# Moving the first gate's modulation rows of the second block from an output projection into the attention before it

## The reference, cut to what matters

```python
# first block, layer l
shift, scale, gate = jnp.split((s_lat @ w_mod[l] + b_mod[l])[:, None, :], 3, axis=-1)
...
x = x + gate * y
# second block
mod = jax.nn.silu(c) @ w_mod[l] + b_mod[l]
sh1, sc1, g1, sh2, sc2, g2 = jnp.split(mod, N_MOD, axis=-1)
...
x = x + g1[:, None] * (merged @ w_out[l])
```

## Time and profile before

| | us |
|---|---|
| median of 3 runs | 3005.51 |
| lowest and highest | 2998.6 and 3023.86 |
| time of the profiled execution | 3000.39 |
| its span in the profile | 2998.6 |
| second attention (layer 1), gate tile 1 to gate tile 15 | 1318.86 to 1444.55 |
| its output projection, from the third tile on | 1475.60 to 1556.35 |

### The profile page before, as it was taken

One profiled execution on the slowest core, in us unless ns is written; L12 is line 12 of the kernel. 1 busy time (PEld: TensorE's weight loads), 2 busy tenths in 40 slices (PEclk: granted clock), 3 DMA queues, 4 the chain that ended last, 5 costly groups with the idle time before them and its releaser, 6 DMA issues.

```text
span 2998.6 us, 48547 instructions
## 1 busy us (share of the span) xinstructions
PE 2857.1 (95%) x17809; PEld 2474.9 (83%) x17809; DVE 1784.0 (59%) x3201; ACT 1452.6 (48%) x2227; POOL 1827.7 (61%) x756
## 2 busy tenths in 40 slices
PE   6899999999899799999988999999999999999999
PEld 4688886777778798878877888999987888888888
DVE  2487982799788857548679998772325444442000
ACT  3222222566422532258645787665446555555443
POOL 1244443333333674455665777668787888888998
PEclk9899999999999899999988999999999999999999
DMA  9877321565687797233674444345565766665655
GB/s 400 318 266 271 142 98 68 201 209 187 230 307 289 250 360 283 84 121 119 229 290 134 158 165 152 136 146 176 168 203 174 246 230 232 239 215 191 208 205 188
DMA packets 147414, 621.50 MB, mean 207 GB/s; under 512 B 16288, under 2 KB 17616, under 8 KB 126288
## 3 DMA queue, kind: packets, MB, share of 16 engines
q1 hardware_dynamic: 146128, 614.48, 57.5%
q10 hardware_dynamic: 1152, 5.24, 0.4%
HBM read 617.54 MB, written 2.12 MB: 207 GB/s over the span
## 4 chain that ended last, share of the span: by engine, by line
issue 46%; POOL 29%; PE 24%; POOLq 1%; DVE 0%; DVEq 0%
POOL w_low L690 29%; PE bank L725 16%; PE bank L726 8%; POOLq L685 0%; POOLq L689 0%; POOLq L690 0%; DVE region L1825 0%; DVE region L1828 0%; DVEq L1825 0%; POOLq L2658 0%
## 5 line engine op out<-in xcount | busy, mean ns | idle before, releaser
L690 POOL TENSOR_TENSOR w_low<-raw,w_high 128x1024 fp32r<-128x1024 f32 x752 | 1827.5, 2448 | 1159.9 <-ACT w_high L1197 1156.8
L1197 ACT ACTIVATE w_high<-raw 128x1024 fp32r<-128x1024 f32 x752 | 793.0, 1057 | 794.9 <-PE bank L738 294.4
L736 PE MATMUL bank<-h,w_high 128*128 128x256 f32 (+1 forms) x2816 | 949.8, 337 | 15.6 <-POOL w_low L690 12.5
L737 PE MATMUL bank<-h,w_high 128*128 128x256 f32 (+1 forms) x2816 | 935.9, 332 | 0.0
L738 PE MATMUL bank<-h,w_low 128*128 128x256 f32 (+1 forms) x2816 | 935.6, 332 | 0.0
L736 PEld LDWEIGHTS bank<-h,w_high 128*128 128x128 f32 x2816 | 538.0, 191 | 92.7 <-issue 25.0
L725 PE MATMUL bank<-h,w_high 128*128 128x512 f32 x1664 | 583.9, 395 | 8.4 <-DVE h L1791 4.2
L738 PEld LDWEIGHTS bank<-h,w_low 128*128 128x128 f32 x2816 | 537.7, 191 | 51.0
L737 PEld LDWEIGHTS bank<-h,w_high 128*128 128x128 f32 x2816 | 538.3, 191 | 50.1 <-issue 0.7
L726 PE MATMUL bank<-h,w_low 128*128 128x256 f32 x1664 | 467.8, 281 | 0.0
L725 PEld LDWEIGHTS bank<-h,w_high 128*128 128x128 f32 x1664 | 313.5, 188 | 80.6 <-POOL w_low L690 4.6
(11 more groups left out here) (256 smaller groups left out, 3506.8 us busy)
## 6 DMA issues: line engine op xcount, KB each, us to landing
raw<-in_w_in SPq DMA_DIRECT2D x344, 512.0 KB, 3.6
raw<-in_w_up SPq DMA_DIRECT2D x176, 512.0 KB, 3.5
region<-in_w_rows SPq DMA_DIRECT2D x71, 1024.0 KB, 7.4
row_extra<-in_w_rows SPq DMA_DIRECT2D x57, 1024.0 KB, 6.9
raw<-in_w_out SPq DMA_DIRECT2D x96, 512.0 KB, 5.6
raw<-in_w_down SPq DMA_DIRECT2D x96, 512.0 KB, 3.4
row_extra<-in_w_half_rows SPq DMA_DIRECT2D x64, 512.0 KB, 4.3
region<-in_w_mods SPq DMA_DIRECT2D x28, 1024.0 KB, 9.6
```

Source lines behind the costliest of these rows:

```text
L690: nc.gpsimd.tensor_tensor(WL[s][:, part], RAW[s][:, part], WH[s][:, part], ALU.subtract) \
L736: nc.tensor.matmul(bank[:, 0:n], WH[slot][:, w], h, start=first and j == 0, stop=False)
L737: nc.tensor.matmul(bank[:, 0:n], WH[slot][:, w], l, start=False, stop=False)
L1197: return nc.scalar.activation(out, in_, func, **kw)
```

## The change

The 16 MB of rows for `g1` leave the stage `out1` and become a stage `att1`: 32 half rows, two behind each of the 16 steps of the second attention, in the manner of `att0`. The host lays them out as half rows. `ROW_ATT0`, the two halves of `ROW_EXTRA`, are the places again, and the conditioning vector goes into `ROW_OUT`, half of it before row 0 and the other half before row 16. SP's loop over units 40 to 53 is written out, with one unit behind each pair of rows; `w_out1` now goes by the plain loop of pairs. The output projection has no rows any more. The core of the diff:

```diff
-    ROW_STAGES = {... "out1": (ROW_OUT1, 18), "up": (ROW_UP, 18)}
+    ROW_STAGES = {... "att1": (ROW_ATT0, 32), "up": (ROW_UP, 18)}
...
+        def row_att1(e):
+
+            if e % 16 == 0:
+                sp.wait_ge(sem("row_used"), ROW_FIRST["att1"] + e)
+                sp.dma_start(ROW_OUT[:].unsqueeze(1), CONDS[:, 2:3, HALF * (e // 16):HALF * (e // 16 + 1)].broadcast_to([P, 1, HALF])) \
+                    .then_inc(sem("cond_rows"), 16)
+            row_load("att1", e, dram["w_half_rows"][64 + e])
...
+                for g in range(16):
+                    row_att1(2 * g)
+                    row_att1(2 * g + 1)
+                    if g < 14:
+                        one(40 + g)
+                return
...
-            if name == "w_out1":
-                two(0)
-                two(1)
-                row_out1(0)
-                sp.wait_ge(sem("at_y"), 12)
-                row_out1(1)
-                row_out1(2)
-                for t in range(4, 16):
-                    for e in range(t - 1, t + 3 if t == 15 else t):
-                        row_out1(e)
-                    one(t)
-                return
...
+        def rows_att1(e):
+
+            half, m = e // 16, e % 16
+            if m == 0:
+                dve.wait_ge(sem("cond_rows"), 65 + 16 * half)
+            place = row_landed("att1", e)
+            total = mod_col(128 + m, 2) if half else ROW_PART[:, m:m + 1]
+            V.scalar_tensor_tensor(place, place, 1.0, ROW_OUT[:], ALU.mult, ALU.mult, accum_out=total) \
+                .then_inc(sem("row_used"), 1)
+            if e == 31:
+                row_bias(ROW_ALL["att1"], 128, 16, 2, 3, 0).then_inc(sem("row_out"), 1)
...
-                if l == 0:
-                    rows_att0(2 * g)
-                    rows_att0(2 * g + 1)
+                for e in (2 * g, 2 * g + 1):
+                    rows_att0(e) if l == 0 else rows_att1(e)
...
-            else:
-                for e in range(3):
-                    rows_out1(e)
...
-                elif n < 15:
-                    rows_out1(3 + n)
```

More of the change, by code:

```diff
@@ L98, in lay_out @@
     out["w_rows"] = np.concatenate([rows_of(early, 0, 2), rows_of(early, 1, 2), rows_of(mods[96:128]),
-                                    rows_of(mods[128:144], 0, 2), rows_of(mods[128:144], 1, 2),
                                     rows_of(mods[176:192], 0, 2), rows_of(mods[176:192], 1, 2),
                                     *(rows_of(late, q, 4) for q in range(4))])
-    rows = rows_of(mods[144:176])
-    out["w_half_rows"] = np.concatenate([rows[:, :, :HALF], rows[:, :, HALF:]])
+    rows, more = rows_of(mods[144:176]), rows_of(mods[128:144])
+    out["w_half_rows"] = np.concatenate([rows[:, :, :HALF], rows[:, :, HALF:], more[:, :, :HALF], more[:, :, HALF:]])
     order2 = list(range(24, 32)) + list(range(24)) + list(range(32, 64))
@@ L341, in build @@
     ROW_IN1 = [ROW_EXTRA[:], *r2(4096, 6144)]
-    ROW_OUT1 = [ROW_EXTRA[:], *r2(0, 4096)]
     ROW_UP = [ROW_EXTRA[:]]
-    ROW_STAGES = {"in0": (ROW_IN0, 34), "att0": (ROW_ATT0, 64), "out0": (ROW_OUT0, 36), "in1": (ROW_IN1, 33), "out1": (ROW_OUT1, 18), "up": (ROW_UP, 18)}
+    ROW_STAGES = {"in0": (ROW_IN0, 34), "att0": (ROW_ATT0, 64), "out0": (ROW_OUT0, 36), "in1": (ROW_IN1, 33), "att1": (ROW_ATT0, 32), "up": (ROW_UP, 18)}
     ROW_FIRST, ROW_LANDED = {}, {}
@@ L532, in row_out0 @@
             else:
-                row_load("out0", e, dram["w_rows"][96 + 8 * (e // 9) + e % 9 - 1])
+                row_load("out0", e, dram["w_rows"][80 + 8 * (e // 9) + e % 9 - 1])
         def row_in1(e):
@@ L540, in row_in1 @@
                 row_load("in1", e, dram["w_rows"][32 + e - 1])
-        def row_out1(e):
-            if e % 9 == 0:
-                row_cond("out1", e, slice(2, 3), e // 9, 2)
-            else:
-                row_load("out1", e, dram["w_rows"][64 + 8 * (e // 9) + e % 9 - 1])
+        def row_att1(e):
[4 more added lines that the diff above has]
+            row_load("att1", e, dram["w_half_rows"][64 + e])
         def row_up(e):
@@ L553, in row_up @@
             else:
-                row_load("up", e, dram["w_rows"][80 + 8 * (e // 9) + e % 9 - 1])
+                row_load("up", e, dram["w_rows"][64 + 8 * (e // 9) + e % 9 - 1])
         row_in0(0)
```

## The result

The changed kernel takes 3140.54 us (median of 4 runs, 3134.75 to 3146.8) against 3014.69 for the kernel before in the same comparison (2998.6 to 3025.66): a ratio of 1.042, 95% interval 1.036 to 1.048. The forecast was 3142. The profiled execution took 3146.8 us with a span of 3145.0, against 3000.39 and 2998.6 before. By the profiles the loss is 146 us, by the medians 126: the execution profiled before was near the fastest of its kernel and the one profiled after was the slowest of its four.

What follows compares the result with a forecast made beforehand. PE, busy for 95% of the span, was taken to bound the kernel before; after the change, a ring of waits the second attention. Profiled 3000.4 + 146 (ring) - 4.4 (output projection) = 3142 us; range 3098 to 3165.

Steps and rivals of the forecast that it cites:

- The ring: Second attention: rows, weights' landing, ACT, DVE's combination, rows wait in a circle once a step; 38.8 us a head against 18.0.
- 14 turns: Second attention, tiles 2 to 15 bound as seven pairs: 21.8 us for odd steps, 17.0 for even.
- the +146 of the sum: Second attention: seven pairs, each 38.8 us instead of 18.0, add 146 us.
- the landing: Second attention: weights land 7.5 us behind the last row sum, 8.7 for the second half.
- the clock's 21 us: Second attention: PE's clock may fall when idle; 1.5 us a step, 21 us, allowed in the range alone.
- the last link: End of the second attention: unit 54, first of `w_out1`, behind row 31, awaited by ACT ahead of `gate(14)`; one of the 14.
- where the tiles stand: Second attention: sign that gate tiles would stand 17 and 22 us apart in turn.
- Output projection: Without its 18 rows, PE's waits fall by 2.4 us for POOL and 2.0 behind the last residual, 4.4 together.
- Landings of 5 us (3107): Rival, second attention: the circle closes but weights land 5.0 us behind the sum; 35 us less, 3107; chance 0.29.
- An open ring with DVE as the limit (3011): Rival, second attention: ACT isn't held, DVE limits; 0 to 30 us added, 3011 in the middle; chance 0.08.
- no loss (2996): Rival: rows fit whole into DVE's idle time in the second attention, only the 4.4 us gain remains; 2996, chance 0.03.

Runs made afterwards that it cites:

- The ring alone: Kernel before, rows unmoved, with one wait more: SP asks for unit 40+x only after DVE's combination of step x-1; 3068.8 us, ratio 1.018.
- the sums: Changed kernel with each row sum of the second attention taking 8 columns instead of 1024 (gate wrong); 3098.5 us, ratio 1.029.
- the run without rows: Kernel before with the 18 rows of the output projection left out, transfers and sums (gate wrong); 3003.32 us, ratio 0.998.
- lead two: Changed kernel, but SP asks for units 40 and 41 before the first rows and unit 42+g behind rows 2g and 2g+1; 3037.43 us, ratio 1.010.
- lead of two, short sums: Changed kernel with weights asked for two units earlier against the rows and each row sum taking 8 of 1024 columns (gate wrong); 3002.82 us, ratio 0.999.

## Why the prediction was right

**The ring.** Forecast as 14 turns of 19.4 us in the mean, 271.6 in all; measured 267.9, so +142.2 against the +146 of the sum. Its terms: the landing is 7.0 behind a release against 7.5 forecast; from landing to landing the steps of the head read above are 21.2 and 16.6 us against 21.8 and 17.0. The ring alone, the landing and the sums were each shown by a run, and the parts add up to within 0.2 to 0.6 us a turn.

**How much of the number is luck.** The mechanism and the length of a turn were forecast; that 3142 lies 1.5 us from the median of 3140.5 is luck. The sum put 141.6 us on top of the profiled execution, the profiles put 134 down to the change, and the medians differ by 126. Thirteen turns of 18.7 us instead of 19.4 and a last one of 24.5 cancel in part, and the medians are of executions that differ by up to 27 us for one kernel. The top of the range has a slip besides: the sum and the clock's 21 us are 3163, not 3165.

**Not as forecast: the last link.** I took unit 54 as one of the 14. It is longer, 24.5 us from tile 14 to tile 15. Four rows stand ahead of it, 28 to 31, and row 31 waits for the use of row 29. Row 28 was asked for at 1568.13, and the release at 1569.25 asks for row 29 and not for weights. DVE, with nothing else to do, waits for both and sums them, and only as their places come free are rows 30 and 31 asked for (1572.81 and 1574.76), and behind them the weights, at 1575.43:

```profile
1569.17 0.48 DVE L2107 SCALAR_TENSOR_TENSOR region<-bank,sg_sb,region 128x256 f32<-128x256 f32 x1
1571.55 1.22 DVE L2055 SCALAR_TENSOR_TENSOR row_extra<-row_extra,row_product 128x1024 f32<-128x1024 f32 x1 [1.90 <-DMA row_extra<-in_w_half_rows]
```

That is some 5 us more, beside shorter turns everywhere else.

**Not as forecast: where the tiles stand.** I said that gate tiles would stand 17 and 22 us apart. They stand 18.1 and 19.6 apart in most heads (once 21.4, where the second half of the conditioning vector lies ahead of the weights in the queue): the table load ahead of the gate's copy falls on one kind of step only (not between 1385.94 and 1386.90 above), which shifts every second tile inside the ring. The period of a head was right, 38.1 from tile 3 to 13 against 38.8.

**Output projection.** Forecast -4.4. The traces show -4.2 in the stretch and -6.2 from its first product to the next stage's; PE's waits for POOL of 2.9 came down to 0.5 as forecast, and for DVE from 4.5 to 3.4, not to 2.5. The times of the run without rows, -6 with an interval that holds 0, don't settle the size; its trace has -5.3.

**The clock.** It fell to 0.77 in the stage, and as forecast that lay beside the ring: in the turn above PE's tile ends at 1395.77, before the next weights let ACT go on at 1402.57. No run separates it.

**Rivals.** Landings of 5 us (3107) are refuted by the 7.0 measured. An open ring with DVE as the limit (3011) and no loss (2996) are refuted for this order. But once the ring is opened they are the right pictures of what comes next: at lead two DVE's turns with POOL bound the stage (1.010), and without the turns nothing is left of the loss in the time.

## What to carry to other kernels

On a queue that serves in order, ask of each transfer that waits for a consumer what stands behind it, and follow that back to the same consumer: if the way closes and the circle is longer than a step of the busiest engine, the stage runs at the length of the circle however idle the engines are. Distance opens it, here two units of lead, and it costs no data. Count DVE work with two SBUF inputs beside POOL's at the length it has under turns, not at its own, before filling idle time with it; and leave the work out altogether once, to see what moving it can gain at most.

## What the runs showed of the hardware that I had not expected

One half unit of weights lands 3.3 us after its issue in the kernel before, where the next half is asked for 2.8 us later. It takes 4.1 in the ring alone, where the two halves are issued 0.4 us apart and no row is near, 4.0 with two half rows behind the halves as well, and 7.0 with two half rows of the same size issued just ahead of them. So the rows behind the weights cost next to nothing here, and the rows ahead of them 3 us.

A small DVE instruction can be held by POOL as well: sums of 8 columns took 0.16 us in the median and 2.36 at most, and the scaling of the combination, whose only full-size input is one tile, took 1.79 us at 1390.27 beside a split of POOL, against 0.55 elsewhere.

PE's granted clock was 0.77 of full in the mean in the attention of the changed kernel, where PE waited 100 us for ACT, and 0.88 in the ring alone, where it waited 38; with the waits gone (lead of two, short sums) it was 0.99 again.
